# A layer of retention and windowed attention on one core: attention by 64-query blocks over their 192 keys, probabilities turned by four loads

## The chip, the core and the metric

One NeuronCore of a Trainium2 chip runs the whole program. The metric is the device time of one execution in microseconds (us). TensorE is called PE here, VectorE DVE, ScalarE ACT, GpSimd POOL, SyncE SP; SP issues nearly all transfers, in program order. Matrices lie in SBUF with 128 partitions; PE writes to eight PSUM banks of 128 x 512 float32.

## The reference, cut to what matters

One layer over 4096 prompt frames and 64 sample frames, width 1024. A modulated RMSNorm feeds one input projection whose columns go to a retention group (4 heads) and to a windowed attention group (8 query heads of 64, two key/value heads, a learned sink per query head). Both are gated, concatenated, projected and added to the residual, and a last RMSNorm follows. The attention works in chunks of 64 queries, each against the 192 keys of its own and the two earlier chunks:

```python
CHUNK = 64; WINDOW = 128; ATT_HEAD_DIM = 64; ATT_Q_HEADS = 8; ATT_KV_HEADS = 2

def _sink_attend(q, k, v, sink, mask):
    s = jnp.einsum('...qhgd,...khd->...hgqk', q, k).astype(jnp.float32) * (ATT_HEAD_DIM ** -0.5)
    if mask is not None:
        s = jnp.where(mask, s, -jnp.inf)          # only keys before position 0 are masked
    sk = sink.reshape(ATT_KV_HEADS, ATT_GROUP)[:, :, None, None]
    m = jnp.maximum(jnp.max(s, axis=-1, keepdims=True), sk)
    p = jnp.exp(s - m)
    denom = jnp.sum(p, axis=-1, keepdims=True) + jnp.exp(sk - m)
    return jnp.einsum('...hgqk,...khd->...qhgd', (p / denom).astype(v.dtype), v)
```

## The kernel before, in words

The program has two phases over 33 tiles of 128 rows (tile 32 holds the last rows and the 64 sample rows). Phase A does norm, projection and retention; it ends near 905 us of the span. Phase B does the attention, the output projection and the final norm. In both, five instruction streams are written out by hand and meet only through semaphores; the order on each engine is the order of the code. `phase_tiles` unrolls the first four slots and the last ones and loops over pairs of slots between.

A dense product is split in high and low parts (float32r): `dense` (L1245) makes three passes of 8 matmuls. A slot of phase B handles three tiles at once on PE, in this order (`slot_b` of the PE block): `scores` of tile t-1 (L1418), `dense_kv` of tile t (24 matmuls of 256 columns), the query projection into `qv_b` and the gate projection into `kg_b` (24 of 512 columns each), the output projection of tile t-2 into `out0_b` and `out1_b` (48 of 512 columns), then `weigh` of tile t-1 (L1439).

`scores` makes 24 float32r matmuls, always two at a time on the upper and the lower 64 rows of the array (`tile_position=(g * HD, 0)`): 128 queries of a head against all 256 keys of this tile and the one before. The result fills the four banks `s_banks`. On DVE `mask_max` (L1076) adds a mask and takes the row maximum in one pass, four times a half, from PSUM into `p_in`; two small operations (L1082, L1085) make the bias. On ACT `softmax` (L775) takes the exponential from `p_in` into `s_row` in the order in which it is to be stored.

The probabilities must be turned (keys into partitions). DVE turns only within blocks of 32 x 32, so the blocks change places through memory: SP stores `s_row` by four transfers a half (`store_blocks`, L489), pieces of 1 KB, loads it back in one transfer (`p_back`, L514), and DVE turns the blocks (`turn_p`, L1090). The queries and keys (`aqk_out` L489, `aqk_in` L509, turned at L1190), the gate (`g_scratch`, L576, turned at L1207) take the same way. Other operands (`yr_in`, and in phase A `xp`, `q_row`) are stored whole and loaded by `load_blocks` (L402): four transfers, each for 32 partitions, in pieces of 128 bytes.

`weigh` multiplies the turned probabilities with the values: 8 float32 matmuls of 256 columns (16 matmul instructions in the trace, two for each), on the left and the right 64 columns of the array, over all 256 keys, into `qv_b`. DVE multiplies the result with the gate (L1131), which PE's next query projection waits for (`ya_done`).

SP's order in a slot of phase B: load of `hf`, stores of the two halves of p, `p_back` 0, `aqk_out`, `p_back` 1, store of the gate, `aqk_in`, store of y, `load_blocks` of `yr_in`, load of the gate into `a_gate`, load of x. DVE's order: gate product L1131, `mask_max` twice, low part L1139, final norm L1145, turn and split of the retention output (L1103 to L1113), reciprocals and gate scaling (L1154 to L1162), second gate step L1172, `turn_p` 0, low part of the next `hf` (L894), `turn_p` 1, turn of queries and keys L1190, their low parts (L1193, L1199), `out0_b` times the gate (L1219, `o0_read`), residual (L1222), turn of the gate (L1207), `out1_b` times the gate (L1227), residual (L1229).

Between the phases SP stores queries and keys of tile 0, loads the last weight piece, then the mask table (L520), the sinks (L523, two transfers of single elements), and then queries and keys of tile 0 (L509).

## Time and profile before

| What | us |
|---|---|
| median of 3 runs (1872.00 to 1873.04) | 1872.92 |
| the profiled execution's own time | 1871.96 |
| its span, first to last instruction | 1870.2 |
| PE busy | 1808.2 (97%) |
| PE weight loads busy | 1496.3 (80%) |
| DVE busy | 1158.4 (62%) |
| ACT busy | 534.0 (29%) |
| POOL busy | 114.9 (6%) |
| share of the 16 DMA engines' time taken by packets | 60.0% |

Phase B's slots follow each other every 28.35 us. A row of the timeline gives the start and the length in us, the engine, the line, the operation with the tile written and the tiles read, the count, and in square brackets the idle time before it and what ended it. PEld is the weight load of PE, SPq the issue of a transfer by SP. The granted clock is given as a share of 2.4 GHz.

### The profile page before, as it was taken

Reading aid. Unit: us, or ns where it says so; the run is one execution under the profiler, and the core shown is the slowest. Engines: PE = TensorE matmul, PEld = TensorE weight load, DVE = VectorE, ACT = ScalarE, POOL = GpSimd, SP = SyncE. Lnnn points to the kernel's source line nnn. Section 1 sums busy time; section 2 is a strip of 40 time slices with the busy share of each in tenths; the row PEclk is TensorE's granted clock in tenths of the full one; section 3 lists DMA queues with packets and bytes.
Section 4 is the critical chain, followed back from the end, with each engine's and each line's share of the span. In section 5 each row is a group of like instructions: output and inputs, shape, how many; then the busy total and the mean of one; then the engine's idle time right before and its main releaser. Section 6 shows DMA issues by size and latency. Waiting matters only on the chain.

```text
span 1870.2 us, 30628 instructions
## 1 busy us (share of the span) xinstructions
PE 1808.2 (97%) x9636; PEld 1496.3 (80%) x9636; DVE 1158.4 (62%) x2742; ACT 534.0 (29%) x1471; POOL 114.9 (6%) x278
## 2 busy tenths in 40 slices
PE   6999999999999999999699999999999999999995
PEld 3787888888888888888588888888888888888874
DVE  3664656665556666567466666675676676666664
ACT  3321222122122222123333332332332333333321
POOL 1000000000000000000000000000000000000000
PEclk8999999999999999999899999999999999999998
DMA  9665555555555555555656656657657557567563
GB/s 373 202 174 167 138 141 133 148 147 125 145 136 129 145 144 135 136 146 152 188 171 190 186 164 197 179 164 204 167 169 208 161 170 206 163 177 198 158 184 103
DMA packets 489519, 314.31 MB, mean 168 GB/s; under 512 B 349554, under 2 KB 424498, under 8 KB 488452
## 3 DMA queue, kind: packets, MB, share of 16 engines
q1 hardware_dynamic: 489476, 313.77, 60.0%
q8 instruction: 23, 0.38, 0.1%
q14 instruction: 20, 0.16, 0.0%
HBM read 183.31 MB, written 130.36 MB: 168 GB/s over the span
## 4 chain that ended last, share of the span: by engine, by line
PE 92%; issue 2%; DVE 2%; DMA 2%; SPq 1%; POOL 0%; ACT 0%; POOLq 0%; DVEq 0%; ACTq 0%
PE bank L1245 79%; PE bank L1439 3%; PE bank L1418 3%; PE bank L1343 2%; PE bank L1329 2%; PE bank L1335 2%; PE bank L1341 2%; DMA aqk_row<-aqk_scratch 1%; DVE wl L319 1%; SPq L402 0%; DMA xn_scratch<-xn 0%; PE bank L1398 0%; SPq L489 0%; DMA out_gate<-gate_scratch 0%; DMA xt<-in_x_prompt 0%
## 5 line engine op out<-in xcount | busy, mean ns | idle before, releaser
L1245 PE MATMUL bank<-wh,hh 128*128 128x512 f32 x1584 | 398.6, 393 | 10.3 <-DVE hh L1045 2.7
L1245 PE MATMUL bank<-wh,hl 128*128 128x512 f32 x1584 | 392.7, 390 | 0.0
L1245 PE MATMUL bank<-wl,hh 128*128 128x512 f32 x1584 | 391.8, 389 | 0.0
L1245 PEld LDWEIGHTS bank<-wh,hh 128*128 128x128 f32 x1584 | 293.2, 189 | 71.8 <-issue 12.3
L1245 PEld LDWEIGHTS bank<-wh,hl 128*128 128x128 f32 x1584 | 298.0, 188 | 62.0
L1245 PEld LDWEIGHTS bank<-wl,hh 128*128 128x128 f32 x1584 | 297.2, 188 | 61.9 <-DVE wl L319 0.3
L703 ACT ACTIVATE hf<-xn,tiny_a 128x128 f32<-128x128 f32 (+1 forms) x248 | 98.6, 480 | 372.0 <-DVE xn L879 372.0
L1172 DVE SCALAR_TENSOR_TENSOR a_gate<-a_gate,bank 128x128 f32<-128x128 f32 x132 | 29.1, 282 | 204.1 <-ACT a_gate L836 204.1
L775 ACT ACTIVATE s_row<-p_in,tiny_b 128x256 f32<-128x256 f32 x264 | 130.9, 499 | 50.0 <-DVE tiny_b L1082 50.0
L1245 PE MATMUL bank<-wh,yh 128*128 128x512 f32 x528 | 132.4, 393 | 7.6 <-DVE yl L1113 7.6
L1245 PE MATMUL bank<-wl,yh 128*128 128x512 f32 x528 | 130.6, 389 | 0.0
L1245 PE MATMUL bank<-wh,yl 128*128 128x512 f32 x528 | 130.4, 389 | 0.0
L1245 PEld LDWEIGHTS bank<-wh,yh 128*128 128x128 f32 x528 | 100.1, 190 | 28.8 <-DVE yl L1113 7.8
L1245 PEld LDWEIGHTS bank<-wl,yh 128*128 128x128 f32 x528 | 99.4, 188 | 20.7
L1245 PEld LDWEIGHTS bank<-wh,yl 128*128 128x128 f32 x528 | 99.1, 188 | 20.6
L1007 DVE SCALAR_TENSOR_TENSOR r_gate<-r_gate,bank 128x512 f32<-128x512 f32 x33 | 22.7, 688 | 135.2 <-ACT r_gate L751 135.2
L1076 DVE CUSTOM_DVE_ANT_0 p_in<-bank,mask 128x256 f32<-128x256 f32 x264 | 96.2, 421 | 1.1 <-issue 1.1
L1090 DVE STREAM_TRANSPOSE s_row<-p_in 128x1024 f32<-128x1024 f32 x66 | 81.6, 1237 | 2.6 <-DMA p_in<-p_scratch 2.5
L924 DVE TENSOR_TENSOR s_t<-bank,decay 128x512 f32<-128x512 f32 x33 | 22.8, 691 | 90.8 <-PE bank L1329 90.8
L836 ACT ACTIVATE a_gate<-bank 128x256 f32<-128x256 f32 x66 | 21.7, 381 | 156.8 <-PE bank L1245 156.8
L664 POOL TENSOR_TENSOR v_prev<-v_row,small 128x128 f32<-128x128 f32 x31 | 12.4, 401 | 857.7 <-PE bank L1439 857.7
L879 DVE STREAM_TRANSPOSE xn<-xp 128x1024 f32<-128x1024 f32 x31 | 38.6, 1246 | 39.5 <-DMA xp<-xn_scratch 39.5
(159 smaller groups left out, 2291.5 us busy)
## 6 DMA issues: line engine op xcount, KB each, us to landing
p_scratch<-s_row SPq DMA_DIRECT2D x264, 128.0 KB, 2.2
p_in<-p_scratch SPq DMA_DIRECT2D x66, 512.0 KB, 4.5
xt<-in_x_prompt SPq DMA_DIRECT2D x64, 512.0 KB, 3.8
h_scratch<-hf SPq DMA_DIRECT2D x33, 512.0 KB, 2.9
hf<-h_scratch SPq DMA_DIRECT2D x33, 512.0 KB, 4.7
out<-xt SPq DMA_DIRECT2D x32, 512.0 KB, 5.0
xn_scratch<-xn SPq DMA_DIRECT2D x31, 512.0 KB, 2.9
xp<-xn_scratch SPq DMA_DIRECT2D x124, 128.0 KB, 2.9
```

The lines of the kernel that those rows point to most:

```text
L703: last = nc.scalar.activation(hf[:, k, lo:P], src, ACT.Identity, bias=h_shift[:, k, c:c + 1], scale=h_scale[:, k, c:c + 1])
L775: nc.scalar.activation(s_row[:, half].rearrange("p b (j s c) -> p b j s c", j=4, s=2)[:, :, j, :, :], p_in[:, half, j, :].rearrange("p (s ...
L879: V.transpose(xn[:, :], xp[:, :]).then_inc(x_turned, 1)
L1076: last = V.tensor_tensor_reduce(out=p_in[:, half, j, :], in0=src, in1=m, scale=1.0, scalar=MASKED, op0=ALU.add, op1=ALU.max, accum_out=s_m ...
L1090: V.transpose(s_row[:, half].rearrange("p b n -> p (b n)"), p_in[:, half].rearrange("p b n -> p (b n)")).then_inc(pt_done, 1)
L1245: ins = mm(out, a[:, k, :], b[:, k, :], start=first and n == part[0] and k == chunks[0], stop=last and n == part[-1] and k == chunks[-1])
L1329: last = mm(qs_b[:, c], k_t[:, c], q_t[:, c], start=True, stop=True)
L1335: last = mm(upd_b[:, c], k_row[:, c], v_dec[:, c], start=True, stop=True)
L1341: mm(out_b[:, c], q_t[:, c], st[:, c], start=True, stop=False)
L1343: last = mm(out_b[:, c], s_t[:, c], v_row[:, c], start=False, stop=True)
L1418: last = mm(s_banks[2 * half + g][:, jl * 2 * P:(jl + 1) * 2 * P], q[rows, 2 * half + jl, :], k[rows, :, :], start=n == 0, stop=n == 2, ti ...
L1439: last = mm(qv_b[cols, half * 2 * P:(half + 1) * 2 * P], v, p_t[:, :, :, g, s, :], start=s == 0, stop=s == 1, tile_position=(0, g * HD))
```

## The change

Each tile's 128 queries are treated as two blocks of 64 (c = 0, 1). The queries' columns are laid out so that the 128 stationary columns of a score matmul hold two heads of one block; the keys are kept in three slots of 128 (`ak_h[P, 3, P]`), the middle slot for even tiles, and the outer two both written for odd tiles (`key_slots`), so that a block's 192 keys lie side by side (`window`). The score matmuls run over 192 columns. The mask is gone, but for tile 0, where DVE overwrites the columns outside. DVE takes the maximum of two rows of 192 from PSUM in one reduction; ACT takes the exponential straight from PSUM into `p_in`. A half is stored as whole rows in one transfer of 384 KB and loaded by `load_blocks` in four transfers of 96 KB, pieces of 128 bytes; DVE turns 768 columns a half in place of 1024. `weigh` makes four matmuls over 128 keys and four over 64 keys, at the four quarters of the array, all of 256 columns, into the left halves of `qv_b` and `out0_b`; it now waits for `ag_done`, for `o0_read` of the same slot and for both halves of `turn_p`. PE's scores wait for the exponentials (`exp_done`) of the tile before. The squares of the final norm go to an SBUF tile of their own. Copies and low parts of the queries are made in two operations each, the gate product in two, the reciprocal in eight. The mask table is no longer loaded, and the sinks come in one transfer of 32 bytes a partition. Its core:

```diff
@@ SP
             def p_back(i, u, half):
                 t = 2 * i + u
-                wait(sp, p_stored[half], 4 * 16 * (t + 1))
-                sp.dma_start(p_in[:, half].rearrange("p b n -> p (b n)"), p_dram[2 * t + half]).then_inc(p_loaded[half], 16)
+                wait(sp, p_stored[half], 16 * (t + 1))
+                load_blocks(p_in[:, half].rearrange("p b n -> p (b n)"), p_dram[2 * t + half], p_loaded[half])
...
-            sp.dma_start(mask[:, :, :], mask_tab).then_inc(fixed_loaded, 16)
-            with nc.allow_non_contiguous_dma(reason="eight sinks, in the heads' order of the pairs"):
-                for g in range(2):
-                    sp.dma_start(neg_sink.rearrange("p (j g) -> p j g", g=2)[:, :, g],
-                                 sink[:, 4 * g:4 * g + 4].partition_broadcast(P)).then_inc(fixed_loaded, 16)
+            sp.dma_start(sinks, sink.partition_broadcast(P)).then_inc(fixed_loaded, 16)
...
-                        store_blocks(p_dram[2 * (t - 1) + half], s_row[:, half], p_stored[half])
+                        sp.dma_start(p_dram[2 * (t - 1) + half], p_in[:, half].rearrange("p b n -> p (b n)")
+                                     ).then_inc(p_stored[half], 16)
@@ ACT, softmax
-                wait(act, pv_ready, 2 * t)
-                for j in range(4):
-                    h = 4 * half + j
-                    nc.scalar.activation(s_row[:, half].rearrange("p b (j s c) -> p b j s c", j=4, s=2)[:, :, j, :, :],
-                                         p_in[:, half, j, :].rearrange("p (s b c) -> p b s c", s=2, b=4), ACT.Exp,
-                                         bias=s_bias[:, h:h + 1], scale=SCORE_SCALE, accum_out=row_sum[:, h:h + 1])
+                wait(act, pt_done, n - 2)
+                p_out = p_in[:, half].rearrange("p b n -> p (b n)")
+                for g in range(2):
+                    for c in range(2):
+                        m = 4 * half + 2 * g + c
+                        keys = slice(3 * HALF * c, 3 * HALF * (c + 1))
+                        nc.scalar.activation(p_out[:, (2 * g + c) * 3 * HALF:(2 * g + c + 1) * 3 * HALF],
+                                             s_banks[2 * half + g][:, keys], ACT.Exp, bias=s_bias[:, m:m + 1],
+                                             scale=SCORE_SCALE, accum_out=sums[:, m, 0:1])
@@ DVE, mask_max -> row_max
-                for j in range(4):
-                    h = 4 * half + j
-                    src = s_banks[2 * half + j % 2][:, (j // 2) * 2 * P:(j // 2 + 1) * 2 * P]
-                    last = V.tensor_tensor_reduce(out=p_in[:, half, j, :], in0=src, in1=m, scale=1.0, scalar=MASKED,
-                                                  op0=ALU.add, op1=ALU.max, accum_out=s_max[:, h:h + 1])
+                for g in range(2):
...
+                    m = 4 * half + 2 * g
+                    last = V.tensor_reduce(s_max[:, m:m + 2], s_banks[2 * half + g][:, 0:6 * HALF].rearrange("p (c k) -> p c k", c=2),
+                                           mybir.AxisListType.X, ALU.max)
@@ PE, scores
-                    wait(pe, s_masked, 2 * (t - 1) + half + 1)
-                    for jl in range(2):
+                    wait(pe, exp_done, 2 * (t - 1) + half + 1)
+                    for c in range(2):
                         for n, (q, k) in enumerate(((aq_h, ak_h), (aq_h, ak_l), (aq_l, ak_h))):
                             for g in range(2):
                                 rows = slice(g * HD, (g + 1) * HD)
-                                last = mm(s_banks[2 * half + g][:, jl * 2 * P:(jl + 1) * 2 * P], q[rows, 2 * half + jl, :],
-                                          k[rows, :, :], start=n == 0, stop=n == 2, tile_position=(g * HD, 0))
+                                last = mm(s_banks[2 * half + g][:, c * 3 * HALF:(c + 1) * 3 * HALF],
+                                          q[rows, 2 * half + c, :],
+                                          window(k, rows, u, c), start=n == 0, stop=n == 2, tile_position=(g * HD, 0))
@@ PE, weigh
-                for half in range(2):
-                    wait(pe, pt_done, 2 * t + half + 1)
-                    p_t = s_row[:, half].rearrange("p i (l g s r) -> p l i g s r", l=2, g=2, s=2)
-                    for s in range(2):
-                        for g in range(2):
-                            cols = slice(g * HD, (g + 1) * HD)
-                            v = v_rows[u][:, cols] if s == u else v_prev[:, cols]
-                            last = mm(qv_b[cols, half * 2 * P:(half + 1) * 2 * P], v, p_t[:, :, :, g, s, :],
-                                      start=s == 0, stop=s == 1, tile_position=(0, g * HD))
-                    last.then_inc(pv_ready, 1)
+                wait(pe, ag_done, t + 1)
+                wait(pe, o0_read, t)
+                wait(pe, pt_done, 2 * t + 2)
+                p_t = s_row[:, :, :, :].rearrange("p h b n -> p h (b n)").rearrange("p h (g k n) -> p h g k n", g=2, k=3)
+                for c in range(2):
+                    v = v_rows[u] if c else v_prev
+                    for g in range(2):
+                        cols = slice(g * HD, (g + 1) * HD)
+                        mm(weighed(i, t, c)[cols, :], v[:, cols], p_t[:, :, g, 2 * c, :], start=True, stop=False,
+                           tile_position=(0, g * HD))
+                for g in range(2):
+                    cols = slice(g * HD, (g + 1) * HD)
+                    for c in range(2):
+                        rows = slice(c * HALF, (c + 1) * HALF)
+                        v = v_prev if c else v_rows[u]
+                        last = mm(weighed(i, t, c)[cols, :], v[rows, cols], p_t[rows, :, g, 1, :], start=False, stop=True,
+                                  tile_position=(c * HALF, g * HD))
+                last.then_inc(pv_ready, 1)
```

## Rows read from the trace of the kernel before

**Rows 1.** The page's chain of work that ended last, shares by line.
```profile
PE bank L1245 79%; PE bank L1439 3%; PE bank L1418 3%; PE bank L1343 2%; PE bank L1329 2%; PE bank L1335 2%; PE bank L1341 2%; DMA aqk_row<-aqk_scratch 1%; DVE wl L319 1%; SPq L402 0%; DMA xn_scratch<-xn 0%; PE bank L1398 0%; SPq L489 0%; DMA out_gate<-gate_scratch 0%; DMA xt<-in_x_prompt 0%
```

**Rows 2.** Busy time by stretch, one slot: us, engines, PEclk, DMA share, GB/s.
```profile
1311.50:1339.85 28.35, 28.35 (x161) 23.36 (x161) 18.30 (x50) 9.75 (x32) 1.34 (x4) 1.00 0.65 180
```

**Rows 3.** PE's waits, whole span: us in total, times, longest.
```profile
PE bank L1418 <- DVE ak_l L1199: 13.7, 1, 13.7
...
PE bank L1245 <- DVE yl L1113: 7.6, 1, 7.6
```

**Rows 4.** Timeline of PE from weigh through scores to the query projection.
```profile
1307.93 0.65 PE L1439 MATMUL bank<-s_row,v_prev 128*64 128x256 f32 x4
...
1309.81 0.39 PE L1418 MATMUL bank<-ak_h,aq_h 64*128 64x256 f32 x2
1310.03 0.28 PE L1418 MATMUL bank<-ak_l,aq_h 64*128 64x256 f32 x2
1310.15 0.28 PE L1418 MATMUL bank<-ak_h,aq_l 64*128 64x256 f32 x2
...
1311.43 1.21 PE L1245 MATMUL bank<-wkvh,hh 128*128 128x256 f32 x8
...
1314.40 2.00 PE L1245 MATMUL bank<-wh,hh 128*128 128x512 f32 x8
```

**Rows 5.** Timeline of PE near the start: four 32-column groups of the array.
```profile
21.15 1.06 PE L1267 MATMUL bank<-stage,k_t 128*32 128x512 f32 x8 [1.37 <-DMA stage<-in_w_ada]
```

**Rows 6.** Groups of PE weight loads by form: busy us, mean ns, idle before.
```profile
L1418 PEld LDWEIGHTS bank<-ak_h,aq_l 64*128 64x128 f32 x264 | 25.7, 191 | 0.0
...
L1439 PEld LDWEIGHTS bank<-s_row,v_prev 128*64 128x64 f32 x264 | 17.5, 136 | 12.9 <-issue 5.6
```

**Rows 7.** Timeline of SP's issues in one slot of phase B.
```profile
1315.10 4.20 SPq L489 DMA_DIRECT2D p_scratch<-s_row  x8
...
1320.93 1.81 SPq L489 DMA_DIRECT2D aqk_scratch<-aqk_row  x4
1322.84 0.38 SPq L514 DMA_DIRECT2D p_in<-p_scratch  x1
...
1325.43 0.37 SPq L509 DMA_DIRECT2D aqk_row<-aqk_scratch  x1
```

**Rows 8.** Timeline of SP in phase A: a load by 128-byte pieces.
```profile
513.71 2.92 SPq L402 DMA_DIRECT2D q_row<-q_scratch  x4
```

**Rows 9.** Line L509 from 980 to 1790 us: issue to landing.
```profile
DMA to landing us min/median/max: 3.9/4.2/5.0
```

**Rows 10.** Timeline of DVE, same slot: turn of queries, first read of out0_b.
```profile
1330.42 0.80 DVE L1190 STREAM_TRANSPOSE aqk_f<-aqk_row 128x640 f32<-128x640 f32 x1
...
1333.01 0.68 DVE L1219 TENSOR_TENSOR yr_f<-bank,out_gate 128x512 f32<-128x512 f32 x1
```

**Rows 11.** DMA queue in 509 to 511 us: packets, MB, share of 16 engines.
```profile
q1 hardware_dynamic: 1982, 0.25, 79.4%
```

**Rows 12.** Timeline between the phases: SP's issues and DVE.
```profile
900.26 1.53 SPq L523 DMA_DIRECT2D tiny_b<-in_sink  x2
...
901.84 1.01 SPq L509 DMA_DIRECT2D aqk_row<-aqk_scratch  x1
...
909.11 2.29 DVE L319 TENSOR_TENSOR wl<-stage,wh 128x2048 fp32r<-128x2048 f32 x1 [3.94 <-ACT wh L315]
...
916.09 0.84 DVE L1190 STREAM_TRANSPOSE aqk_f<-aqk_row 128x640 f32<-128x640 f32 x1 [4.69 <-DMA aqk_row<-aqk_scratch]
```

**Rows 13.** DMA queue in 908 to 912 us, columns as in Rows 11.
```profile
q1 hardware_dynamic: 403, 0.00, 4.5%
```

**Rows 14.** Group of the masked maximum by form: busy us, mean ns, idle before.
```profile
L1076 DVE CUSTOM_DVE_ANT_0 p_in<-bank,mask 128x256 f32<-128x256 f32 x264 | 96.2, 421 | 1.1 <-issue 1.1
```

**Rows 15.** The chain near the end, in order of time: start, us, what.
```profile
1816.16 2.97 DMA a_gate<-g_scratch
...
1829.29 13.02 PE bank L1245 x48
```

More of the change, by code:

```diff
@@ L161, in build_program @@
         sink_arg = tiny_b[:, 24:32]
-        sink_exp = tiny_b[:, 32:40]
-        row_sum = tiny_b[:, 40:48]
-        den = tiny_b[:, 48:56]
-        rden = tiny_b[:, 56:64]
+        sums = tiny_b[:, 32:48].rearrange("p (n s) -> p n s", s=2)
+        den = tiny_b[:, 56:64]
+        rden = tiny_b[:, 64:72]
+        sinks = tiny_b[:, 72:80]
         xts = [xt0, xt1]
@@ L355, in y_of, with key_slots, window, pair_of @@
             return (hh0, hl0) if static(i) and t == SAMPLE else (yh, yl)
+        def key_slots(ak, u):
+            return ak[:, 0:3:2, :] if u else ak[:, 1:2, :]
+        def window(ak, rows, u, c):
+            first = P * u + HALF * c
+            return ak[rows, :, :].rearrange("p s r -> p (s r)")[:, first:first + 3 * HALF]
+        def pair_of(aq, half):
+            return aq[:, 2 * half:2 * half + 2, :].rearrange("p c (t l r) -> p (c t) l r", t=2, l=2)
+        def quarter(cols, b):
+            return cols[32 * b:32 * (b + 1)]
+        def queries_f(half):
+            return aqk_f[:, :, 2 * half:2 * half + 2, :]
+        def weighed(i, t, c):
+            second = kg_b if static(i) and t == SAMPLE else out0_b
+            return (second if c else qv_b)[:, 0:KV]
         def ag_bank(i, t):
@@ L662, in slot_b @@
                 if not static(i) or 1 <= t < SAMPLE:
[L663 removed]
+                    wait(pool, pv_ready, t)
                     nc.gpsimd.tensor_tensor(v_prev[:, :], v_rows[1 - u][:, :], zero.to_broadcast([P, P]),
@@ L1061, in _, with row_max @@
             dve.wait_ge(out_ready, SAMPLE + 1)
-            def mask_max(i, u, half):
+            def row_max(i, u, half):
                 t = 2 * i + u
@@ L1088, in turn_p @@
                 t = 2 * i + u
-                wait(dve, p_loaded[half], 16 * (t + 1))
+                wait(dve, p_loaded[half], 4 * 16 * (t + 1))
+                wait(dve, pv_ready, t)
                 V.transpose(s_row[:, half].rearrange("p b n -> p (b n)"),
@@ L1153, in slot_b @@
                     wait(dve, gate_scaled, t - 1)
-                    V.tensor_tensor(den, row_sum, sink_exp, ALU.add).then_inc(den_done, 1)
+                    V.tensor_reduce(den, sums, mybir.AxisListType.X, ALU.add).then_inc(den_done, 1)
                     wait(dve, den_done, t)
-                    V.reciprocal(rden, den).then_inc(rden_done, 1)
+                    for c, b, l in itertools.product(range(2), repeat=3):
+                        last = V.reciprocal(quarter(rden, 2 * c + b).rearrange("p (h l g) -> p h l g", h=2, l=2)[:, :, l, :],
+                                            quarter(den, 2 * b + l).rearrange("p (h g c) -> p h g c", h=2, g=2)[:, :, :, c])
+                    last.then_inc(rden_done, 1)
                     wait(dve, rden_done, t)
```

102 lines of the change are left out of this document (52 added, 50 removed).

## The prediction, made before the changed kernel ran

> **What bounds the kernel now.** Read the chain that ended last first: four fifths of the span are the dense product's line on PE, and the lines of scores and weigh have 3% each [rows 1]. Then the busy time by stretch: in a slot of phase B PE is busy for 28.35 of 28.35 us, at a granted clock of 1.00 (2.4 GHz), while DVE works 18.30 and ACT 9.75, and the DMA engines are taken for 65% [rows 2]. Then PE's waits: the view has no row between 975 and 1795 us, and the long ones stand at the phase change (13.7 us, for the low part of the first keys) and near the end (7.6 us, for the split of the retention output) [rows 3]. So three things count: PE's own work in a slot, whether what feeds PE still comes in time, and the two waits. DVE and ACT savings inside a slot are worth nothing by themselves.
>
> **PE, weigh.** In the timeline weigh runs from 1307.93 to 1309.81, 1.88 us for 16 instructions; the two column halves go in pairs, so that is 8 steps of 0.215 us (256 columns at two cycles a column are 0.213) and 0.16 for entering and leaving [rows 4]. The change keeps 16 instructions of 256 columns: the four products over 128 keys make 4 steps; the four over 64 keys sit in the four quarters of the array and make 2 steps if all four run together, 4 if only two do. No row shows quarters. The nearest is the ada product: four 32-column groups, 8 instructions of 512 columns in 1.06 us [rows 5]. A step of 512 columns is 0.43; two steps and 0.2 of tail fit, four steps (1.7) don't. So four tiles of one height run together, and I take quarters to do so too: 2 steps fewer, -0.43. Against it stands one more change of tile shape. Its price, from weigh to scores and into the dense product: scores takes 1.62 for 12 steps of 0.12, so 0.1 to 0.2 goes at each change [rows 4]; I take 0.15. Weigh: -0.28 a slot, bounds -0.43 and +0.2. The skill's page "TensorEngine Tiling (Array Packing)", section Key Properties, says that changing the tiling mode, not just the tile, drains the engine; the 0.1 to 0.2 is what that drain shows as here.
>
> **PE, scores.** 12 steps of two matmuls, 0.12 us each (1310.03 to 1310.15) [rows 4]. A step streams 256 columns, 0.107 us at one cycle a column; with 192 it would be 0.080. But each step also needs two new weight sets of 128 columns. A load of 128 columns takes 191 ns, one of 64 columns 136 [rows 6]: 55 ns for 64 columns, so 107 to 110 ns of array time for 128, whatever lies in the rest. Dense passes of 256 columns, with one 128-column load each, keep the same 0.12 (24 in the 2.97 us from 1311.43 to 1314.40) [rows 4]. So I expect the load to hold the step at 0.12 once the stream is shorter: gain 0, bounds -0.32 (12 x 0.027) and the rival below. The skill's page "TensorE: Matmul & The Clock Gate" says both: section LDWEIGHTS, that a load costs its columns over 1.2, whatever the rows, 107 ns here, with which the two rows agree; section Back-to-back issue gap, that a stream costs N/2.4 + 2.5 ns, 82.5 in place of 109, which would give those -0.32 a slot.
>
> **Will PE be fed?** The new wait is weigh's for `o0_read`; behind it on PE stand the next scores and all dense work. Out0 is ready early, so it hangs on DVE's order: turn of queries (L1190), low parts, then L1219. L1190 waits for `aqk_in`, and SP issues that behind `p_back` 1. SP in a slot: `aqk_out` 1.81 us at 1320.93, `p_back` 1 0.38, gate store, `aqk_in` at 1325.43 [rows 7]. Four 128-byte-piece loads take 2.92 us of SP [rows 8], so `aqk_in` slips by 2.5, to 1328.0 (up to 3.1, an estimate: these four issues beside heavier traffic). `p_back` 0 slips nothing: the stores fall from 8 issues in 4.20 us to 2 [rows 7], so its 2.92 end before `aqk_out`, which waits for PE. Landing takes 4.2 (3.9 to 5.0) [rows 9]: 1332.2, where DVE came to L1190 at 1330.42 without waiting. L1219 began at 1333.01 and took 0.68 [rows 10]; +1.8, and 0.3 for low parts cut in two, gives `o0_read` at 1335.8, against a weigh due at 1307.93 + 28.35 = 1336.28. Slack 0.5 at the median, nothing left with the slower issue, -0.3 with the slowest landing. I take 0.1 a slot on average, bounds 0 and 0.8. The gains on PE lie outside this stretch and don't move it.
>
> DMA time: 1982 packets of 128 bytes took 79.4% of 16 engines for 2 us, 12.8 ns each [rows 11]. 6144 a slot are 4.9 us. Even if the larger pieces taken away had cost nothing, the share would be (18.4 + 4.9) / 28.35 = 82%: room. The small pieces cost SP issue time, not queue time.
>
> DVE loses four masked passes a half (mean 421 ns) [rows 14] and takes two reductions of 384 columns, 0.4 to 0.6 each by the 0.68 for 512 columns from PSUM [rows 10]; turning 768 columns for 1024 saves 0.6, seven more reciprocals cost about 1. It has 10 us idle in a slot [rows 2]; worth 0 there. ACT's exponentials read PSUM now, which no exponential's row shows; with 192 columns for 256 and 18 us idle in a slot [rows 2] even a longer one costs nothing, and `exp_done` of the tile before lies some 20 us ahead of the next scores. Cost 0; were that cover gone, PE would wait for it.
>
> **Phase change.** Between 908 and 912 us the DMA queue handles 403 packets at 4.5% of the engines and next to no bytes [rows 13]: single elements, the sinks of L523. `aqk_in` was issued at 901.84 behind them and landed at 916.09, when DVE had waited 4.69 us [rows 12]. With the sinks as one small transfer and no mask it should land before 911.4. Then DVE is the next late: its last weight split (L319) ends at 909.11 + 2.29 = 911.40 [rows 12]. Gain 4.7, and 0.3 from the shorter `turn_p` 0 ahead of L894: -5.0, bounds -5.3 and -2 (if something else queues). The clock's return is the same in either.
>
> **The end.** In the last slots SP is itself on the chain: the gate load is issued at 1816.16, 2.97 us later DVE starts a run of work that releases PE at 1829.29 [rows 15]. `p_back` 1 puts it off by 2.5 to 3.1; the run holds both maxima, eight passes with 0.345 between starts, about 4.0 us with the small operations, 2.6 after. So +2.8 - 1.4 = +1.4, bounds 0 and +3.
>
> **The sum.** Against the profiled execution, 1871.96 (span 1870.2, 1.8 outside): weigh 33 x -0.28 = -9.2; scores 0; stall 29 x 0.1 = +2.9; phase change -5.0; end +1.4. Total -9.9: **1862.0**. The median of the runs lies 1.0 above the profiled one, so the ratio would be about 0.995. Own range of this case: 1855 to 1868.
>
> **Rivals.** *The scores do shorten* with their columns: 33 x -0.32 = -10.6, 1851.5. For it: a full dense pass shows that loads hide behind streams; against it the 55 ns between 64 and 128 columns, and no row with a stream shorter than a 128-column load. Chance 0.12.
>
> *Quarters don't run together*: 33 x +0.2 in place of -9.2, so about 1871.96 + 6.6 - 5.0 + 1.4 = 1875, 1870 with the lower price of the change of shape. For it: no row has both halves of rows and of columns; against it the four groups of rows 5. Chance 0.15.
>
> *SP makes a new wait.* If `aqk_in` slips by 3.1 and lands after 5.0, `o0_read` comes 0.8 late in each slot: 29 x 0.8 = 23 in place of 2.9, 1882. It decides once `o0_read` passes 1336.3. For it: half a microsecond of slack on four terms; against it, a load of DMA no higher than before at that moment. Chance 0.13, 1868 to 1890.
>
> *The narrow float32r matmul is slower*, the slower end: no float32r row in this trace has under 256 columns, so that 192 columns run at one cycle is unproven. At two cycles a step is 0.171 for 0.12, 12 x 0.05 = +0.6 a slot, about 1883; at the four cycles that a float32 pair costs in weigh (0.43 for 256 columns), 0.33, +2.5 a slot, 1945. Then the change's saving of columns is a loss. For it only the missing row, against it that 512 and 256 columns cost one cycle each. Chance 0.15, half of it at the high price.
>
> **How the numbers follow.** Forecast 0.45, the rest as above. A difference of 0.2% (3.7 us) is about what a measurement here can tell from none. Faster: the forecast nearly whole (0.43), the shorter scores 0.12, 0.05 from the other cases: 0.60. Same: 0.02 + 0.09 (quarters) + 0.04 (SP) + 0.01 = 0.16. Slower: quarters 0.04, SP 0.06, narrow 0.14: 0.24. The range 1849 to 1884 leaves out the high price (0.08), the worst SP slots and a little below.
>
> **What would show it.** Slot period: 28.2 by the forecast, 27.8 with shorter scores, 28.5 with pairs only, 28.8 and more with a slow narrow matmul. Steps in scores of 0.12, not 0.09 or 0.17 and more; four instructions of weigh starting together. In PE's waits no row for the first read of `out0_b` worth over 3 us in all, or the SP case is on. DVE's turn of queries after the phase change at 911.4. The prediction is wrong if the narrow step or the quarters differ from their nearest rows; both are extrapolated.

## The result and the profile after

| What | before | after |
|---|---|---|
| median of the runs, us | 1872.98 | 1855.92 |
| range, 4 runs each | 1872.0 to 1873.21 | 1853.78 to 1857.88 |
| profiled execution, us | 1871.96 | 1855.76 |
| its span | 1870.2 | 1854.0 |
| DMA packets in the span | 489519 | 657424 |
| share of the DMA engines' time | 60.0% | 59.7% |

The ratio is 0.991, with an interval of 0.9892 to 0.9927: the change is faster, by 17.1 us between the medians and 16.2 between the profiled executions, where the forecast was 9.9 below the profiled execution. Where it comes from shows first in one slot of phase B, the row that answers to [rows 2] (same columns):

```profile
1299.90:1327.88 27.98, 27.98 (x163) 22.93 (x162) 19.05 (x47) 9.17 (x33) 1.33 (x4) 1.00 0.62 159
```

A slot takes 27.98 us for 28.35, still all of it on PE at a granted clock of 1.00. DVE's busy time swings from slot to slot (16.93, 19.05 and 18.21 us in three that follow each other); over the steady part it is 18.1 us a slot, before 18.2, and PE does not wait for it there. Next the chain of PE in the same slot (start, length, what), and the timeline of the first instructions of each kind, for [rows 4]:

```profile
1298.29 1.01 PE bank L1481 x8
1299.31 0.59 PE bank L1488 x8
1299.90 1.52 PE bank L1458 x24
```

```profile
1299.24 0.43 PE L1488 MATMUL bank<-s_row,v_row 64*64 64x256 f32 x1
...
1299.83 0.36 PE L1458 MATMUL bank<-ak_h,aq_h 64*128 64x192 f32 x2
1300.02 0.27 PE L1458 MATMUL bank<-ak_l,aq_h 64*128 64x192 f32 x2
1300.14 0.27 PE L1458 MATMUL bank<-ak_h,aq_l 64*128 64x192 f32 x2
...
1301.14 0.28 PE L1458 MATMUL bank<-ak_h,aq_l 64*128 64x192 f32 x2
```

Weigh is 1.01 + 0.59 and its gaps, 1.61 from start to start, for 1.88; the four instructions over 64 keys begin within 0.02 us of each other. Scores take 1.52 for 1.62: from 1300.02 to 1301.14 there are ten steps, 0.112 each; before, the same ten (1310.03 to 1311.22) took 0.119 each, and the first step was 0.22 for 0.19. 0.27 + 0.10 = 0.37, the whole gain of the slot.

PE's waits, for [rows 3]:

```profile
PE bank L1285 <- DVE yl L1143: 9.0, 1, 9.0
PE bank L1458 <- DVE ak_l L1238: 8.7, 1, 8.7
```

The wait for the first keys fell from 13.7 to 8.7, the one near the end grew from 7.6 to 9.0. No wait of weigh for `out0_b`'s first read stands in the list. The rows that should have shown one are SP's, the landing of L537's loads, and DVE's, in one slot (for [rows 7] to [rows 10]):

```profile
1310.99 1.97 SPq L517 DMA_DIRECT2D aqk_scratch<-aqk_row  x4
1313.06 2.91 SPq L430 DMA_DIRECT2D p_in<-p_scratch  x4
1316.15 2.00 SPq L517 DMA_DIRECT2D g_scratch<-a_gate  x4
1318.34 0.37 SPq L537 DMA_DIRECT2D aqk_row<-aqk_scratch  x1
```

```profile
DMA to landing us min/median/max: 3.2/3.4/3.7
```

```profile
1321.77 0.84 DVE L1230 STREAM_TRANSPOSE aqk_f<-aqk_row 128x640 f32<-128x640 f32 x1 [1.88 <-DMA aqk_row<-aqk_scratch]
...
1324.80 0.69 DVE L1259 TENSOR_TENSOR yr_f<-bank,out_gate 128x512 f32<-128x512 f32 x1
```

`aqk_in` is issued 20.1 us after the weighing began, before 17.5: a slip of 2.6. DVE now waits 1.88 us for it, which it did not before. But the load lands after 3.4 where it took 4.2, so the read of `out0_b` ends at 1325.49, 0.7 before the next weighing at 1326.20. DVE's new wait is real and covered. How well covered is to be read with care: a weighing that does wait for this read starts 0.25 us behind the read's end, so of the 0.71 in this slot 0.46 is slack. Over the 30 steady slots the distance is 0.92 in the median (slack 0.67) and at least 0.71, but for the last two: there it is 0.26 and 0.25, and these slots take 28.14 and 28.17 us for 27.98.

Between the phases (DVE's timeline, then the chain), for [rows 12]:

```profile
909.05 2.29 DVE L321 TENSOR_TENSOR wl<-stage,wh 128x2048 fp32r<-128x2048 f32 x1 [3.63 <-ACT wh L317]
911.26 0.84 DVE L1230 STREAM_TRANSPOSE aqk_f<-aqk_row 128x640 f32<-128x640 f32 x1
```

```profile
898.79 8.29 DMA stage<-in_w_out
```

The queries' turn no longer waits for a load; it starts as the last split of the weight ends, and that hangs on the load of the last weight piece. The first scores start at 914.19 for 918.86.

The end, chain of the kernel before, then of the changed one (for [rows 15]):

```profile
1829.29 13.02 PE bank L1245 x48
...
1842.33 0.70 DVE yr_f L1227
...
1844.64 5.73 PE bank L1245 x24
1850.37 1.90 PE bank L1439 x16
```

```profile
1801.54 3.69 DMA a_gate<-g_scratch
...
1814.45 18.96 PE bank L1285 x72
1833.41 1.01 PE bank L1481 x8
...
1838.83 5.52 DMA out_gate<-gate_scratch
```

Before, PE ran 48 dense matmuls, stood until DVE had read and ACT had squared the last half, and ran 24 more: 21.1 us to the weighing. After, the 72 run in one go, 19.0 us. The squares lie in a tile of their own, and PE's bank no longer waits for them. That gain was not in the sum.

**The ledger.** The lead of the changed kernel, event by event: first scores 4.7 (918.86 to 914.19); weighing of the second tile 5.3 (967.77 to 962.48); the weighing 30 slots later 16.0 (1818.17 to 1802.21); PE's resumption at the end 14.8; the last weighing 17.0; the span 16.2. So: 5 before the steady slots, 10.7 in them (30 x 0.37, less the 0.35 of the two that waited), -1.1 and +2.1 at the end, and 0.8 given back behind the last weighing, where the load of `out_gate` took 5.52 us for 4.41. That last item is a chance of this profile and not of the change: in six other traces of the changed kernel or a variant of it the same load took 4.1 to 4.3 us, in three 5.5 to 6.0, and in the repeated changed kernel 4.26.

### The profile page after: what moved, and what is told of

Read it like the earlier page. It is cut to its first block, busy times and chain, and to the rows that moved or that the text cites. A ratio compares the mean times of both kernels' runs of the same rounds, so it can differ in the third digit from the quotient of the medians.

```text
span 1854.0 us, 30536 instructions
## 1 busy us (share of the span) xinstructions
PE 1796.5 (97%) x9636; PEld 1482.0 (80%) x9636; DVE 1154.1 (62%) x2588; ACT 516.7 (28%) x1504; POOL 116.7 (6%) x278
## 2 busy tenths in 40 slices
DMA packets 657424, 296.64 MB, mean 160 GB/s; under 512 B 551378, under 2 KB 592530, under 8 KB 656356
## 3 DMA queue, kind: packets, MB, share of 16 engines
q1 hardware_dynamic: 657380, 296.08, 59.7%
## 4 chain that ended last, share of the span: by engine, by line
PE 92%; DVE 2%; issue 2%; DMA 2%; SPq 1%; ACT 0%; POOL 0%; POOLq 0%; DVEq 0%; ACTq 0%
PE bank L1285 80%; PE bank L1458 3%; PE bank L1481 2%; PE bank L1383 2%; PE bank L1369 2%; PE bank L1375 2%; PE bank L1381 2%; PE bank L1488 1%; DVE wl L321 1%; SPq L430 1%; DMA xn_scratch<-xn 0%; DMA stage<-in_w_out 0%; PE bank L1438 0%; SPq L517 0%; DMA out_gate<-gate_scratch 0%
## 5 line engine op out<-in xcount | busy, mean ns | idle before, releaser
L1212 DVE SCALAR_TENSOR_TENSOR a_gate<-a_gate,bank 128x128 f32<-128x128 f32 x132 | 29.1, 282 | 194.9 <-ACT a_gate L863 194.9
L802 ACT ACTIVATE p_in<-bank,tiny_b 128x192 f32<-128x192 f32 x264 | 107.6, 428 | 28.4 <-DVE tiny_b L1111 28.4
L874 ACT ACTIVATE aq_h<-aqk_f 128x256 fp32r<-128x256 f32 x66 | 23.9, 410 | 186.5 <-DVE aqk_f L1230 186.5
L1105 DVE TENSOR_REDUCE tiny_b<-bank 128x2 f32<-128x384 f32 x132 | 67.6, 552 | 4.4
L1120 DVE STREAM_TRANSPOSE s_row<-p_in 128x768 f32<-128x768 f32 x66 | 64.1, 970 | 2.6 <-DMA p_in<-p_scratch 2.6
```

The lines of the kernel that those rows point to most:

```text
L802: nc.scalar.activation(p_out[:, (2 * g + c) * 3 * HALF:(2 * g + c + 1) * 3 * HALF], s_banks[2 * half + g][:, keys], ACT.Exp, bias=s_bias[: ...
L1105: last = V.tensor_reduce(s_max[:, m:m + 2], s_banks[2 * half + g][:, 0:6 * HALF].rearrange("p (c k) -> p c k", c=2), mybir.AxisListType.X, ...
L1120: V.transpose(s_row[:, half].rearrange("p b n -> p (b n)"), p_in[:, half].rearrange("p b n -> p (b n)")).then_inc(pt_done, 1)
```

## The experiments

The numbers in brackets behind a ratio are its interval. Each is against the kernel before on the same chip.

**The sinks alone.** The kernel before, with one edit between the phases:

```diff
-                for g in range(2):
-                    sp.dma_start(neg_sink.rearrange("p (j g) -> p j g", g=2)[:, :, g],
-                                 sink[:, 4 * g:4 * g + 4].partition_broadcast(P)).then_inc(fixed_loaded, 16)
+            sp.dma_start(sinks, sink.partition_broadcast(P)).then_inc(fixed_loaded, 16)
```

> The kernel before with one part of the change alone: the eight sinks come as one transfer of 32 bytes a partition in place of two of single elements, and DVE puts them in order; the mask table is still loaded. If the single elements held the first keys back (my theory), the wait of DVE's L1190 for aqk_row after the phase change (4.69 us) goes and the first scores start 4 to 4.7 us earlier: the kernel is 4.3 us faster, about 1868.6, and the slots keep their 28.35 us. If the 384 KB mask table was to blame (rival), the time stays at 1873 and the wait stays over 3 us.

Measured: 1866.76 us for 1872.94, ratio 0.9971 (0.9959 to 0.9982), so 3.4 to 7.7 us. Its DVE between the phases:

```profile
909.52 2.29 DVE L320 TENSOR_TENSOR wl<-stage,wh 128x2048 fp32r<-128x2048 f32 x1 [3.35 <-ACT wh L316]
911.73 0.84 DVE L1188 STREAM_TRANSPOSE aqk_f<-aqk_row 128x640 f32<-128x640 f32 x1
```

The wait of 4.69 us is gone and the same split is next late. The load of the queries lands 8.1 us after its issue, before 14.2. The edit alone is worth what the step said (4.4 us at the first scores, 918.86 to 914.50). Two small transfers of single elements were about a third of what the whole change brings.

**The mask's load put back.** The changed kernel with a transfer of 384 KB ahead of the sinks:

```diff
+            sp.dma_start(xt1[:, 0:4 * 3 * HALF], x_prompt[0:P, 0:4 * 3 * HALF]).then_inc(fixed_loaded, 16)
             sp.dma_start(sinks, sink.partition_broadcast(P)).then_inc(fixed_loaded, 16)
...
-                    dve.wait_ge(fixed_loaded, 16)
+                    dve.wait_ge(fixed_loaded, 32)
```

> The changed kernel with a dead load of the mask's size (128 rows of 3 KB) put back ahead of the sinks; nothing else. My theory: its 1.7 us of queue time end before DVE is free for the first keys (911.3), so no more than 0.5 us is lost and the time is that of the changed kernel, 1855.9 within 1. Rival, the mask had a share in the 4.7: 2 us slower or more, with DVE's turn of the first queries waiting on its transfer.

Measured: 1855.58, ratio 0.9906 (0.9889 to 0.9922). The first scores wait 8.0 us, no more than the 8.7 of the changed kernel. That the mask is no longer loaded gave nothing; the bytes were never the trouble.

**Quarters of the array, or halves.** The changed kernel, its last four products of weigh over all 128 rows. The number of instructions and of columns stays:

```diff
-                for g in range(2):
-                    cols = slice(g * HD, (g + 1) * HD)
-                    for c in range(2):
-                        rows = slice(c * HALF, (c + 1) * HALF)
+                for c in range(2):
+                    for g in range(2):
+                        cols = slice(g * HD, (g + 1) * HD)
                         v = v_prev if c else v_rows[u]
-                        last = mm(weighed(i, t, c)[cols, :], v[rows, cols], p_t[rows, :, g, 1, :], start=False, stop=True,
-                                  tile_position=(c * HALF, g * HD))
+                        last = mm(weighed(i, t, c)[cols, :], v[:, cols], p_t[:, :, g, 1, :], start=False, stop=True,
+                                  tile_position=(0, g * HD))
```

> The changed kernel with the four products over 64 keys replaced by four over all 128 rows, in pairs by column half, as before (it computes other sums for the middle keys, so its attention values differ; the same 16 instructions of 256 columns). My theory: weigh goes back from 1.61 to 1.88 us, slots from 27.98 to 28.25, 33 x 0.27 = 8.9 us slower, 1865. It prices the quarters: two steps of 0.215 less one more change of tile shape of 0.16. Rival, the shape change costs nothing or all of the gain: 1.72 or 2.04 us, that is 1860 or 1870.

Measured: 1863.14, ratio 0.995 (0.9933 to 0.9967). The chain:

```profile
1301.98 1.01 PE bank L1481 x8
1302.99 0.86 PE bank L1487 x8
1303.86 1.52 PE bank L1458 x24
1330.23 1.01 PE bank L1481 x8
```

Weigh is 1.88 again and the slot 28.25. The median stands 7.6 above the 1855.58 of the run with the mask's load on the same chip, where 33 x 0.27 = 8.9 were due. So the four quarters do run together, and the two steps less (0.43) are paid with 0.16 for the further change of shape.

**What holds the step of the scores.** Two runs. In the changed kernel the low-part passes stream 128 of 192 columns, in the kernel before 192 of 256:

```diff
+                                w = 3 * HALF if n == 0 else P
...
+                                          window(k, rows, u, c)[:, 0:w], start=n == 0, stop=n == 2, tile_position=(g * HD, 0))
```

```diff
+                                w = 2 * P if n == 0 else 3 * HD
...
+                                          k[rows, :, :].rearrange("p s n -> p (s n)")[:, 0:w],
```

> The changed kernel, in which the two low-part passes of every score product stream only the first 128 of their 192 key columns (this leaves out the low-part products of the last 64 keys of each window). In the changed kernel's trace the step between score instructions is 0.111 us. Theory A (the step is held by the 128-column weight load, 0.107 to 0.110 us in the rows): the step stays at 0.11 and the time at the changed kernel's, 1855.9, within 1. Theory B (the step is held by the streamed columns, 192 of them at 2.4 GHz are 0.080 and what lies around them): 8 of the 12 steps of a slot shorten by up to 0.027 to 0.04, so 0.2 to 0.3 less in each of 32 slots, 1846 to 1849.

> The kernel before, in which the two low-part passes of every score product stream 192 of their 256 key columns (this leaves out the low-part products of 64 keys). In the kernel before the steps are 0.118 us. If the streamed columns held that step (256 at 2.4 GHz are 0.107) and the weight load holds a shorter one (0.111 in the changed kernel), the three steps of a group take together between 3 x 0.111 and 3 x 0.118, nearer to the first: 24 matmuls in 1.52 to 1.57 us for 1.62. If something else held 0.118 in the old layout (the 192 adjacent columns, the order of the heads), it stays at 0.118 and 1.62.

Measured, the first: 1856.25 us, ratio 0.9902 (0.9887 to 0.9917), while the changed kernel had 1858.19 and 0.9912 (0.9899 to 0.9926) on this chip. Its steps:

```profile
1301.67 0.31 PE L1459 MATMUL bank<-ak_h,aq_h 64*128 64x192 f32 x2
1301.81 0.24 PE L1459 MATMUL bank<-ak_l,aq_h 64*128 64x128 f32 x2
1301.89 0.28 PE L1459 MATMUL bank<-ak_h,aq_l 64*128 64x128 f32 x2
1302.00 0.30 PE L1459 MATMUL bank<-ak_h,aq_h 64*128 64x192 f32 x2
```

A group of three still takes 0.33, 0.11 a step, though it streams 448 columns where it streamed 576. Within the group the starts shift, the sum does not move (the slot takes 27.93 us for 27.98). The second, in one execution of 1874.41 us:

```profile
1311.82 1.54 PE bank L1419 x24
```

1.54 for 1.62, and its slots follow each other every 28.27 us. So with 256 columns the step (0.119; the expectations have 0.118) falls when columns are taken away, to 0.113 over a group of 640 columns; with 192 and with 448 over three it stays at 0.111 to 0.112.

The first scores of phase B show the floor alone, since behind its long wait PE runs them at the lower clock, a granted 0.50 (the changed kernel's stretch, then two groups of the run with the narrow low parts):

```profile
914.20:916.80 2.60, 2.60 (x24) 2.60 (x24) 1.29 (x6) 0.00 (x0) 0.00 (x0) 0.50 0.00 0
```

```profile
916.01 0.50 PE L1459 MATMUL bank<-ak_h,aq_h 64*128 64x192 f32 x2
...
917.29 0.50 PE L1459 MATMUL bank<-ak_h,aq_h 64*128 64x192 f32 x2
```

There a step takes 0.213 us in all four kernels: with 256 columns (919.22 to 921.35 for ten steps), with 256 and twice 192, with 192 (914.49 to 916.63 for ten), and with 192 and twice 128 (six steps from 916.01 to 917.29). If the columns held it, 192 would be 0.160 at one a cycle of 1.2 GHz. So below 256 columns the step does not depend on them at either clock, and it nearly doubles when the clock is halved; half of 0.213 is 0.107. That is the 107 to 110 ns that the two loads of [rows 6] gave for a weight set of 128 columns. The starts of the weight loads point the same way: they lie even, 0.111 apart at the full clock and 0.213 at the lower, with the narrow low parts too, where the starts of the matmuls shift. The floor is shown to lie there; that it is the load's own time still rests on these two arguments, since no run changed the load's width. The section LDWEIGHTS of the Trainium skill's page "TensorE: Matmul & The Clock Gate" gives 107 ns for such a load, and 0.112 at the full clock agrees. Its section Back-to-back issue gap gives a formula that it calls the isolated gap, without the weight load: 109 ns for 256 columns, where the trace has 119, and 82.5 for 192, where it has 112. Below the load's time the formula for the stream does not decide.

**How much slack is left on SP.** The changed kernel, with two of the four loads of `p_back` 1 cut in two by partitions, so that SP issues six transfers for four:

```diff
-                for j in range(4):
+                for j in range(cut):
+                    for r0 in (0, 16):
+                        sp.dma_start(dst[32 * j + r0:32 * j + r0 + 16, :].rearrange("r (k i c) -> r k i c", i=4, c=32),
+                                     src.rearrange("(i r) (k j c) -> r k i j c", r=32, j=4, c=32)[r0:r0 + 16, :, :, j, :]
+                                     ).then_inc(loaded, 16)
+                for j in range(cut, 4):
```

> The changed kernel, in which two of the four loads that take the second half of the probabilities apart are each cut into two by partitions, so SP issues six transfers where it issued four: 1.46 us more of SP ahead of the query-key row's load, at 0.73 each. Theory A (the read of the attention output starts late enough to hold TensorE once its slack is used up; after the change the trace has 0.7 to 0.9 us of slack and no wait): a wait of 0.5 to 0.8 us ahead of the weighing in each of 27 to 29 slots, 14 to 23 us, so 1870 to 1879. Theory B (slack is larger than the rows show, since VectorE's splits absorb it): no wait, 1855.9 within 1.

Measured: 1889.14 us, ratio 1.0086 (1.0068 to 1.0103): slower than the kernel before, and worse than expected. The wait and a slot's rows:

```profile
PE bank L1484 <- DVE yr_f L1262: 28.4, 31, 1.9
```

```profile
1337.34 0.84 DVE L1233 STREAM_TRANSPOSE aqk_f<-aqk_row 128x640 f32<-128x640 f32 x1 [2.83 <-DMA aqk_row<-aqk_scratch]
...
1340.37 0.68 DVE L1262 TENSOR_TENSOR yr_f<-bank,out_gate 128x512 f32<-128x512 f32 x1
```

The read of `out0_b` ends 29.1 us behind the weighing (1311.97 to 1341.05), in the changed kernel 27.3: 1.8 later, of which the two issues (6 in 4.6 us for 4 in 3.1) are 1.5. Less that slot's slack of 0.46 it is 1.3, and this slot, one of the longest, takes 29.33. The mean of the 30 slots is 28.93, 0.94 more than before, which is 28 of the 31 us between the medians (1858.19 for the changed kernel on this chip); another 3 fall between the first two weighings (28.71 us for 25.64), where PE also waits 1.6 for the second tile's queries. The expectation had 0.5 to 0.8 a slot; the waits are 28.4 us over 31, 0.92 each. So the mechanism of the rival exists just as it was described, its slack is about 0.7 us, and behind it each microsecond costs about 30.

**The squares' wait put back.**

```diff
                     wait(pe, o0_read, t - 2)
+                    wait(pe, fsq_done, t - 2)
...
                     pe.wait_ge(o0_read, t - 1)
+                    pe.wait_ge(fsq_done, t - 1)
```

> The changed kernel with PE's two waits for the last squares (fsq_done) before the products into out0_b put back; the squares themselves stay in SBUF. My theory from the two traces: the waits cost nothing in a slot, but at the end the sample tile's product waits for the squares again, about 2.1 us, as between 1842.3 and 1844.6 in the kernel before: about 1858, slots of 27.98 unchanged, and PE idle ahead of the last 24 dense matmuls. Rival: the 2.1 us came from elsewhere (an earlier residual), then 1856 and no such gap.

Measured: 1859.84, ratio 0.9923 (0.9906 to 0.9939), 4.3 us above the neighbour with 1855.58. The chain at the end:

```profile
1817.44 13.30 PE bank L1285 x48
1830.77 0.70 DVE yr_f L1267
...
1832.75 0.20 ACT squares L839
...
1833.08 5.73 PE bank L1285 x24
1838.81 1.01 PE bank L1481 x8
```

From PE's resumption to the weighing 21.4 us, as in the kernel before (21.1), for 19.0: 2.4 (19.4 in two other traces of the changed kernel: 1.9 to 2.0). So the wait is worth about 2 us. The rest lies elsewhere: two of its slots lost 0.8 us to a wait for the read of `out0_b`, and between the phases the last weight piece landed 9.85 us after its issue, in the changed kernel 8.29. In the ten traces that have that load on the chain it took between 7.7 and 9.9, and a piece of it goes straight into the time; a difference of 1 to 2 us between two single profiles is no more than that.

**The two ends.** What is left there was tried by an edit between the phases (the last splits of the weight behind the queries), two at the end (the gate's load ahead of the residual's rows, the split of the last rows ahead of the maxima), and all three:

```diff
@@ DVE and ACT, first slot: moved behind the low parts (DVE) and the high parts (ACT) of the first queries
-                if static(i) and t == 0:
-                    for n in range(B_OUT_LATE, len(pieces)):
-                        split_lo(dve, n)
...
@@ SP, slot SAMPLE, ahead of the loads of yr_in
+                    sp.wait_ge(g_stored, 4 * 16 * t)
+                    sp.dma_start(a_gates[1 - u][:, :], g_dram[t - 1]).then_inc(g_loaded, 16)
@@ DVE, slot SAMPLE + 1
+                if late:
+                    dve.wait_ge(x1_added, SAMPLE - 1)
+                    split_yr(i - 1, u)
...
+                if late:
+                    row_max(*prev, 0)
+                    row_max(*prev, 1)
```

> The changed kernel with three edits that touch the two ends of the sampling part alone: (1) in the first slot ScalarE's and VectorE's late splits of the weight stand behind the turn and the split of the first queries; the first scores waited 8.7 us, of which the splits hold about 4, so the wait falls to 4.7 to 5.2 and the time by 3.5 to 4; (2) in the last slot the gate's load is issued ahead of the two loads of the residual rows, 1.4 to 2.8 us earlier; (3) in the slot behind it VectorE splits the last rows before it takes the maxima, 1.4 us earlier: the wait of 9.0 us ahead of the last dense products falls by up to 4. If both ends give what they hold: 1855.9 - 3.7 - 4 = 1848, lower bound 1845. Rival: the tail is then held by the weighing of the last slot and its loads (nothing of 2 and 3 is gained): 1852. Rival: a later split of the weight holds the products that need it, and 1 gives nothing: 1852 to 1856.

> The changed kernel as it is, beside the three others on the same chip: 1855.9 within 1, 0.991 of the kernel before.

> The changed kernel with the edit between the phases alone (the last pieces of the weight are split behind the turn and the split of the first queries). The first scores come 3.4 us earlier. Theory A, read in the trace of the kernel that had all three edits: all of it is lost again before the third tile is weighed (the next scores wait 2.5 us for queries that SyncE has not issued earlier, and the first dense product behind that idle time runs 1.8 us slower), so 1855.9 within 1. Theory B: the loss there was chance, and 1.5 to 3.4 us remain, 1852.5 to 1854.4.

> The changed kernel with the two edits at its end alone: in the last slots the gate's load is issued ahead of the two loads of the residual rows, and VectorE splits the last rows before it takes the maxima. From the trace of the kernel that had these two and a third edit between the phases, the end is 4.0 us shorter (from the weighing at 1804.7 to the next at 1836.2, 31.6 us, against 27.6) and nothing is lost elsewhere: 1855.9 - 4 = 1852, 0.989 of the kernel before. Rival: part of the 4 us came from the edit between the phases: 1854 to 1856.

Measured: all three 1854.09, 6 above what both ends together should have given, ratio 0.9891 (0.9876 to 0.9906); the changed kernel again 1858.19, 0.9912 (0.9899 to 0.9926); the first edit alone 1856.48, 0.9915 (0.9902 to 0.9929); the two at the end alone **1851.55, 0.9891** (0.9876 to 0.9906), the lowest median, by its ratio level with all three. The intervals overlap, so the times alone do not part the end's edits from the changed kernel; the traces do. Why the first gives nothing is to be read in its PE:

```profile
912.25 0.53 PE L1458 MATMUL bank<-ak_h,aq_h 64*128 64x192 f32 x2 [4.87 <-DVE ak_l L1235]
932.31 2.07 PE L1285 MATMUL bank<-wkvh,hh 128*128 128x256 f32 x8 [5.23 <-DVE hl L922]
...
940.88 0.36 PE L1458 MATMUL bank<-ak_h,aq_h 64*128 64x192 f32 x2 [1.62 <-issue]
```

The first scores come at 912.25 for 914.19, PE waits 5.2 us for 3.7 at the next product and another 1.6 for the second tile's queries, whose load SP has not issued any earlier. The second tile (the expectations call it the third) is weighed at 964.52, in the repeated changed kernel (first scores 915.01) at 964.63. The gain is all given back. What is late next is SP: in the kernel with all three edits it issues without a pause from 924.3 to the load of the second tile's queries at 934.1, and the next scores hang on that load.

The two edits at the end keep what they bring:

```profile
1808.03 2.08 PE L1295 MATMUL bank<-wh,yh 128*128 128x512 f32 x8 [2.61 <-DVE yl L1183]
1822.81 1.39 PE L1295 MATMUL bank<-wh,hh 128*128 128x512 f32 x4 [3.64 <-DVE yr_f L1269]
```

The wait of 9.0 us has become 2.6 and 3.6, and the two last weighings lie 27.8 us apart (1802.23 to 1830.06), for 31.1 in the changed kernel and 31.6 in its repetition. The new 3.6 invited one more step, DVE's read ahead of the turns of the probabilities:

```diff
+                if late:
+                    read_out0(xts[u])
                 if mid:
                     turn_p(*prev, 0)
```

> As after_end_only, and in the slot behind the last VectorE reads the output projection's first half before it turns the probabilities. In the trace that read began at 1824.5, behind two turns that waited for their loads 2.2 and 1.6 us, and TensorE had waited 3.4 us for it and then ran 24 dense matmuls in 7.3 us at the lower clock (5.4 at the higher). Theory A: TensorE runs on, the weighing comes at 1827.3 in place of 1832.6, and then the gate's turn (1828.4) decides: 4.6 us less, 1847.5. Rival: the second turn of the probabilities, whose load lands at 1823.5, or the gate's load holds the weighing's result, and the clock gives back less: 1850.

Measured: 1853.3, ratio 0.9903 (0.9888 to 0.9918), no gain over the two edits alone (the intervals overlap), its median higher by 1.8. The read is early, and another wait has taken the place of the old:

```profile
1826.80 1.78 PE L1302 MATMUL bank<-wh,hh 128*128 128x512 f32 x4 [4.37 <-DVE yr_f L1284]
```

This is the read of the second half. In the program it stands behind the turn of the gate, whose load landed at 1825.4. The expectation had set the gate's load against the weighing, not against this read.

## Why the prediction was right, and where it was off

**Weigh, forecast -0.28 a slot: right.** Measured -0.27, and both parts of it: -0.43 for two steps less, +0.16 for the change of shape, forecast 0.15. The bounds -0.43 and +0.2 were honest about what no row showed; the four groups of [rows 5] were the row to extrapolate from. The rival of pairs alone is out.

**Scores, forecast 0: the mechanism right, the size off.** Below 256 columns the step stands at the weight load's time, at both clocks. But the step of before was not held by it yet: two neighbouring starts (1310.03 and 1310.15) gave 0.12, ten steps of the same timeline give 0.119, and the floor from [rows 6] was 0.107 to 0.110. "Held at 0.12" took two numbers for equal that the trace tells apart. The step went to 0.112: 12 x 0.007, and 0.02 in the first step, are 0.10 a tile and 3.3 us over 33 tiles. The rival of the full shortening (0.09 a step, slot 27.8) is out: 128 columns did not go below 0.11 either.

**Stall, forecast +0.1 a slot: next to none came.** The slip was forecast at 2.5 to 3.1 and was 2.6. The landing was taken at 4.2 with [rows 9] and was 3.4 (3.2 to 3.7 over 29 loads; a median of 3.4 in six other traces of the changed kernel or a variant too, and still 4.2 in the kernel before with the one transfer of the sinks). That 0.8 is the term that was mis-sized. A smaller one was left out the other way: the 0.25 us from the read's end to the weighing that waits for it. The added 0.3 for the low parts is in the row (1.18 for two instructions and 0.42). So the slack was about 0.7, and two slots used it up, for 0.35 us in all; in the repeated changed kernel three did:

```profile
PE bank L1481 <- DVE yr_f L1259: 0.8, 3, 0.4
```

Against the forecast of 2.9 us that is 2.6 less. Why the load lands sooner no run tells: it is the same transfer, and what stands ahead of it in the queue has changed. To take this rival seriously was sound, as the run with six transfers shows: 1.5 us more on SP a slot cost 31 us, more than the whole change brings.

**DMA time, forecast no trouble: right.** The packets rose by a third, the share in a slot fell from 0.65 to 0.62. The bound of 82% was far off; it had put the pieces that were dropped at nothing, and the bytes fell as well (314 to 297 MB).

**DVE and ACT at 0: right.** The reductions take 0.55 us each, the exponentials from PSUM 0.43 for 0.50; both lie in idle time.

**Phase change, forecast -5.0: right,** in size, in its cause (one sinks' transfer alone gave it) and in what is late next, to 0.1 us (911.26 for a forecast 911.4). That it fits to 0.1 is in part luck: the first scores come at 918.86 and 921.02 in two traces of a kernel that is the one before up to there, and between 913.6 and 916.3 in eight of one that is the changed kernel up to there.

**The end, forecast +1.4: right for the wait, and one term missed.** The wait grew by 1.4, 9.0 for 7.6. What the sum left out is in the diff and in the text on the change: the squares of the final norm go to a tile of their own, so PE no longer waits for them before it fills `out0_b`. The prediction listed that edit and costed it nowhere. It is -2.1 at the one place where PE stood for it. In this pair of profiles 1.1 us in the last load of `out_gate` stand against it, which the other traces show to be chance.

**The sum.** Weigh -8.9, scores -3.3, stall +0.3, phase change -5.0, end +1.4 - 2.1 + 1.1 = +0.4: -16.5, measured -16.2. Against the forecast of -9.9 the errors are 3.3 (scores), 2.6 (stall) and 1.0 (the end), all toward less time, and 0.3 the other way in weigh. The time lay inside the case's own range of 1855 to 1868, but 0.9 us from its edge. That it still lay inside is luck as much as judgement: three terms missed the same way, and the squares' term was in no bound.

**The narrow matmul, chance 0.15: out.** 192 columns took no 0.171 or 0.33 a step but 0.112.

## What to carry to other kernels

When a stream gets shorter, look up what else a step needs and compare the two numbers to the last nanosecond, over many steps and not over two: the step falls only to the larger of them. Follow every edit of the diff to the waits that it removes, also the one that only gives a result a tile of its own. And before adding issues to a queue that many things follow, measure the slack behind it: here 0.7 us a slot stood between a gain of 17 us and a loss.

## What the runs showed of the hardware

- Four products at the four quarters of the array (64 rows x 64 columns each) start within 0.02 us of one another; the next four follow 0.26 us later, where a pair at two column halves follows after 0.215. All that the shape costs beyond its two steps of 0.215 is 0.16 us a tile.
- A step of two float32r products with new weight sets of 128 columns takes 0.119 us with 256 columns each and 0.111 to 0.112 with 192, or 192 and 128 mixed; at the granted clock of 0.50 it takes 0.213 with any of them. No penalty for fewer than 256 columns showed, but the floor of 0.111 would hide one of up to 1.4 times the 0.080 that 192 columns take at one a cycle.
- Two transfers that scatter single elements held the queue so that a load issued 1.6 us behind them landed 14.2 us after its issue, at 4.5% of the DMA engines' time. With the two joined into one transfer of 32 bytes a partition it landed after 8.1, and nothing waited for it.
- 168000 more packets, from pieces of 128 bytes, did not raise the DMA engines' busy share (60.0% to 59.7%), while the bytes fell from 314 to 297 MB.
- The same load at the same place varies from trace to trace: that of the last weight piece took 7.7 to 9.9 us in ten traces, the last one of `out_gate` 4.1 to 6.0 in thirteen. Where the chain hangs on one such load, a single profile carries that spread.
